# A transformer kernel's first block: the compressed attention branch of all heads computed once, with block matrices, instead of slot by slot

## The reference, cut to what matters

```
# 8 heads of 64 in 2 groups of 4 (H, G); n_cmp = 31
kc = compress(k_cmp, pe_k, w1_k, w2_k)          # [31, H, 64]
vc = compress(v_cmp, pe_v, w1_v, w2_v)
s_cmp = einsum('bshgd,bchd->bhgsc', qg, kc) * 64 ** -0.5
mask_cmp = cmp_start + 31 <= pos                # a block counts once it is complete
p_cmp = masked_softmax(s_cmp, mask_cmp)         # over the 31 blocks
o_cmp = einsum('bhgsc,bchd->bshgd', p_cmp, vc)
...
o_slc, o_win = ...      # both reduce to causal attention over all 512 positions here
o = g[..., 0:1] * o_cmp + g[..., 1:2] * o_slc + g[..., 2:3] * o_win
```

## Time and profile before

| what | us |
|---|---|
| median of three runs | 2639.01 (2637.17 to 2639.22) |
| profiled execution | 2638.98 |
| its span, first to last instruction | 2637.1 |
| TensorE busy | 2595.0 |
| VectorE busy | 1574.9 |
| GpSimd busy | 1525.6 |
| ScalarE busy | 850.3 |

### The profile page before, as it was taken

The page is one execution under the profiler, slowest core; times in us unless marked ns, Lnnn a source line. Parts: engine busy times, 40 slices in busy tenths (PEclk is TensorE's granted clock), DMA queues, the critical chain, the costliest instruction groups (busy, mean ns, idle before and its releaser), DMA issues.

```text
span 2637.1 us, 33257 instructions
## 1 busy us (share of the span) xinstructions
PE 2595.0 (98%) x11819; PEld 2081.2 (79%) x11819; DVE 1574.9 (60%) x2192; ACT 850.3 (32%) x1245; POOL 1525.6 (58%) x1820
## 2 busy tenths in 40 slices
PE   8999999999999999999999999999999999999999
PEld 6777777888888876777888888877677788888887
DVE  6666774388483768755574432657874448443375
ACT  5444444223222332355321111134234532111212
POOL 6634345566665754554566655764454456665576
PEclk9999999999999999999999999999999999999999
DMA  5311112222222221222323222232122232222223
GB/s 194 121 49 57 56 58 103 97 96 96 96 96 98 105 107 64 80 95 81 104 82 111 96 96 95 96 112 86 64 80 96 80 104 96 96 96 96 96 97 126
DMA packets 36832, 247.47 MB, mean 94 GB/s; under 512 B 4464, under 2 KB 4848, under 8 KB 7792
## 3 DMA queue, kind: packets, MB, share of 16 engines
q1 hardware_dynamic: 34704, 238.57, 25.8%
q10 hardware_dynamic: 2016, 7.35, 0.8%
HBM read 243.81 MB, written 2.10 MB: 93 GB/s over the span
## 4 chain that ended last, share of the span: by engine, by line
PE 88%; DVE 9%; ACT 1%; issue 1%; POOL 0%; DMA 0%; DVEq 0%; ACTq 0%
PE bank L745 18%; PE bank L747 17%; PE bank L746 17%; PE both L745 10%; PE both L747 10%; PE both L746 10%; PE bank L780 1%; PE bank L1104 1%; PE both L1080 1%; PE both L932 1%; PE bank L918 1%; DVE small L1411 1%; ACT prob L511 0%; PE bank L956 0%; DVE tb L1847 0%
## 5 line engine op out<-in xcount | busy, mean ns | idle before, releaser
L340 POOL TENSOR_TENSOR w_lo<-raw,w_hi 128x256 fp32r<-128x256 f32 x1784 | 1503.3, 874 | 1021.0 <-ACT w_hi L397 1020.5
L397 ACT ACTIVATE w_hi<-raw 128x1024 fp32r<-128x1024 f32 x446 | 469.3, 1057 | 991.7 <-PE bank L747 496.4
L745 PE MATMUL bank<-a_hi,w_hi 128*128 128x512 f32 x1544 | 633.0, 410 | 4.5 <-POOL w_lo L340 4.5
L747 PE MATMUL bank<-a_hi,w_lo 128*128 128x512 f32 x1544 | 604.2, 391 | 0.0
L746 PE MATMUL bank<-a_lo,w_hi 128*128 128x512 f32 x1544 | 603.7, 391 | 0.0
L745 PEld LDWEIGHTS bank<-a_hi,w_hi 128*128 128x128 f32 x1544 | 291.4, 189 | 75.1 <-issue 12.8
L746 PEld LDWEIGHTS bank<-a_lo,w_hi 128*128 128x128 f32 x1544 | 291.8, 189 | 64.1 <-issue 8.5
L747 PEld LDWEIGHTS bank<-a_hi,w_lo 128*128 128x128 f32 x1544 | 291.0, 188 | 62.8
L745 PE MATMUL bank<-y_hi,w_hi 128*128 128x512 f32 x696 | 272.4, 391 | 0.0
L747 PE MATMUL bank<-y_hi,w_lo 128*128 128x512 f32 x696 | 270.9, 389 | 0.0
L746 PE MATMUL bank<-y_lo,w_hi 128*128 128x512 f32 x696 | 270.8, 389 | 0.0
(11 more groups left out here) (299 smaller groups left out, 3043.5 us busy)
## 6 DMA issues: line engine op xcount, KB each, us to landing
raw<-stream SPq DMA_DIRECT2D x223, 1024.0 KB, 4.8
h<-xT SPq DMA_DIRECT2D x8, 256.0 KB, 6.0
h<-xT ACTq DMA_DIRECT2D x1, 2048.0 KB, 8.1
outT<-h SPq DMA_DIRECT2D x8, 256.0 KB, 2.5
h<-decay ACTq DMA_DIRECT2D x1, 1024.0 KB, 4.8
h<-rope ACTq DMA_DIRECT2D x1, 1024.0 KB, 9.2
prob<-pT ACTq DMA_DIRECT2D x2, 512.0 KB, 4.2
par<-par ACTq DMA_DIRECT2D x2, 408.0 KB, 3.1
```

The costliest lines, as they stand in the source:

```text
L340: pool.tensor_tensor(w_lo[:, s, part], raw[:, s, part], w_hi[:, s, part], ALU.subtract).then_inc(lo_done, 1)
L397: act.activation(w_hi[:, s, cols], raw[:, s, cols], ACT.Copy).then_inc(hi_done, 1)
L745: pe.matmul(dst, w_hi[:, s, cols], rhs_hi(k), start=start and k == 0, stop=False)
L747: ins = pe.matmul(dst, w_lo[:, s, cols], rhs_hi(k), start=False, stop=stop and k == nk - 1)
```

## The change

The compressed branch leaves the slots. In head t = 0 it is computed once for all eight heads:

- `kc` becomes a block matrix 128x64: the keys of group 0 in rows 0 to 63 and columns 0 to 30, those of group 1 in rows 64 to 127 and columns 32 to 62. One product of a full 128-row query tile gives the scores of both groups' heads. 16 such products (4 query blocks x 4 tiles) go at j = 0, k = 1.
- VectorE adds the masks, takes the 32 maxima and subtracts them behind `step_probs(0, 0)` (`compressed_shift`); ScalarE takes one exponential of 128x992 in slot 1; VectorE sums, inverts, masks and gates behind `step_probs(0, 1)` (`compressed_probs`).
- At j = 2, k = 1 TensorE transposes the probabilities (8 transposes), ScalarE copies them in two copies; `vc` holds the values of both groups at four row offsets, and at j = 3 to 6, k = 1 one product of 64 rows and 512 columns gives one t's output for both groups, which ScalarE copies to `cmp_out`.
- `attention_out` adds `cmp_out[:, t]` in one more instruction. The value network's transposes and products move from slot 0 to slot 1.

```diff
@@ TensorE
-                if t == 0:
-                    pe.wait_ge(compressed_keys_ready, 1)
...
-                    pe.matmul(b_cmp[:, 0:NCMP], qt[rows, cols], kc[rows, 0:NCMP], start=True, stop=True)
...
-                    pe.transpose(b_cmp[0:NCMP, 0:P], pc[:, 0:NCMP], ident)\
-                        .then_inc(probs_transposed, ptp.up())
...
-                    pe.matmul(b_o[0:DH, col], vc[:, g * DH:(g + 1) * DH], ptc, start=True, stop=False,
-                              skip_group_check=True)
...
+                def compressed_branch(j):
+                    if j == 0:
+                        pe.wait_ge(compressed_keys_ready, 1)
+                        pe.wait_ge(queries_ready, 1)
+                        pe.wait_ge(hidden_copied, 2)
+                        for i in range(QT):
+                            for q in range(QT):
+                                c0 = i % 2 * 256 + q * 64
+                                ins = pe.matmul((b_r0, b_r1)[i // 2][:, c0:c0 + 64],
+                                                m[:, q + 3, i * P:(i + 1) * P], kc, start=True, stop=True)
+                            if i % 2 == 1:
+                                ins.then_inc(cmp_scores_ready, 1)
+                    if j == 2:
+                        pe.wait_ge(cmp_probs_ready, 1)
+                        for pair, dst in enumerate((b_cmp, b_r0)):
+                            for i in range(QT):
+                                c0 = i * 256 + pair * P
+                                ins = pe.transpose(dst[:, i * P:(i + 1) * P], cmp_rows[:, c0:c0 + P], ident)
+                        ins.then_inc(cmp_transposed, 1)
+                    if 3 <= j < 3 + QT:
+                        q = j - 3
+                        if q == 0:
+                            pe.wait_ge(cmp_probs_copied, 2)
+                            pe.wait_ge(compressed_values_ready, 1)
+                        else:
+                            pe.wait_ge(cmp_out_copied, q)
+                        rows = slice(q % 2 * DH, (q % 2 + 1) * DH)
+                        pe.matmul(b_cmp[:, :], vc[rows, :], cmp_turned[rows, q // 2, :], start=True, stop=True)\
+                            .then_inc(cmp_values_ready, 1)
...
-                    if (t, j) == (0, 0) and k in (2, 5):
-                        (hidden_transposes if k == 2 else compress)(1)
+                    if t == 0 and k == 1:
+                        compressed_branch(j)
+                    if (t, j) == (0, 1) and k == 2:
+                        pe.wait_ge(cmp_scores_read, 2)
+                        hidden_transposes(1)
+                    if (t, j) == (0, 1) and k == 5:
+                        compress(1)
@@ ScalarE
-                    softmax_step([(pc[:, 0:NCMP], b_cmp[:, 0:NCMP], 0),
-                                  (prob[:, 0, 0:n], b_s0[:, 0:n], 1),
-                                  (prob[:, 1, 0:n], b_s1[:, 0:n], 2)], DH ** -0.5)
+                    softmax_step([(prob[:, 0, 0:n], b_s0[:, 0:n], 0),
+                                  (prob[:, 1, 0:n], b_s1[:, 0:n], 1)], DH ** -0.5)
...
+            def compressed_branch(j):        # called behind ahead(u0, j), t == 0
+                if j == 1:
+                    act.wait_ge(cmp_shifted, 1)
+                    act.activation(cmp_seen, cmp_seen, ACT.Exp, scale=DH ** -0.5).then_inc(cmp_exp_ready, 1)
+                if j == 2:
+                    act.wait_ge(cmp_transposed, 1)
+                    act.activation(cmp_turned[:, 0, :], b_cmp[:, :], ACT.Copy).then_inc(cmp_probs_copied, 1)
+                    act.activation(cmp_turned[:, 1, :], b_r0[:, :], ACT.Copy).then_inc(cmp_probs_copied, 1)
+                if 3 <= j < 3 + QT:
+                    act.wait_ge(cmp_values_ready, j - 2)
+                    act.activation(cmp_out[:, j - 3, :], b_cmp[:, :], ACT.Copy).then_inc(cmp_out_copied, 1)
@@ VectorE: step_maxima loses the mask and the maximum of the compressed scores, step_probs its two
@@ instructions on pc
+            def compressed_shift():          # behind step_probs(0, 0)
+                for half, src in enumerate((b_r0, b_r1)):
+                    V.wait_ge(cmp_scores_ready, half + 1)
+                    for o in range(2):
+                        i = 2 * half + o
...
+                        ins = V.tensor_tensor(cmp_seen[:, 8 * i:8 * i + 8, :], x,
+                                              seen.unsqueeze(1).to_broadcast([P, 8, NCMP]), ALU.add)
...
+                V.tensor_reduce(cmp_max, cmp_seen, AX.X, ALU.max).then_inc(vector_step, steps.up())
+                V.wait_ge(vector_step, steps.now())
+                V.tensor_tensor(cmp_seen, cmp_seen, cmp_max.unsqueeze(2).to_broadcast([P, 32, NCMP]),
+                                ALU.subtract).then_inc(cmp_shifted, 1)
+
+            def compressed_probs():          # behind step_probs(0, 1)
+                V.wait_ge(cmp_exp_ready, 1)
+                V.tensor_reduce(cmp_max, cmp_seen, AX.X, ALU.add).then_inc(vector_step, steps.up())
...             # reciprocal of 32, four products with the mask's column, two with the gates
+                V.tensor_tensor(cmp_seen, cmp_seen, cmp_scale.unsqueeze(2).to_broadcast([P, 32, NCMP]),
+                                ALU.mult).then_inc(cmp_probs_ready, 1)
...
@@ attention_out
+                V.wait_ge(cmp_out_copied, t + 1)
+                V.tensor_tensor(out_rows, out_rows, cmp_out[rows, t, :], ALU.add)\
+                    .then_inc(vector_step, steps.up())
+                V.wait_ge(vector_step, steps.now())
@@ slot(t, j)
-                if (t, j) == (0, 0):
+                if (t, j) == (0, 1):
                     hidden_out(1)
                 step_probs(t, j)
                 if (t, j) == (0, 0):
+                    compressed_shift()
+                if (t, j) == (0, 1):
+                    compressed_probs()
                     V.wait_ge(compressed, cp.due())
...             # one copy to vc before; now four, to row offsets 0, 32, 64 and 96
```

More of the change, by code:

```diff
@@ L956, in attention_values @@
                             ins = pe.matmul(b_o[rows, col], v_sw[g][:, a, rows], pt[:, half, a * P:(a + 1) * P],
-                                            start=half == 1 and a == 0, stop=a == i, skip_group_check=True)
+                                            start=a == 0, stop=a == i, skip_group_check=True)
                     ins.then_inc(values_added, pv.up())
@@ L1443, in step_probs @@
                 V.wait_ge(exp_ready, ex.due())
-                V.reciprocal(small[:, 12:15], small[:, 4:7]).then_inc(vector_step, steps.up())
+                V.reciprocal(small[:, 12:14], small[:, 4:6]).then_inc(vector_step, steps.up())
                 V.wait_ge(vector_step, steps.now())
-                gate = [gates[:, i, 3 * g + b:3 * g + b + 1] for b in range(3)]
-                V.scalar_tensor_tensor(out=pc[:, 0:NCMP], in0=pc[:, 0:NCMP], scalar=small[:, 12:13],
-                                       in1=cst[:, K_CMPM + i * NCMP:K_CMPM + (i + 1) * NCMP],
-                                       op0=ALU.mult, op1=ALU.mult).then_inc(vector_step, steps.up())
@@ L1450, in step_probs @@
-                V.tensor_scalar(prob[:, 0, 0:n], prob[:, 0, 0:n], small[:, 13:14], gate[1],
+                gate = [gates[:, i, 3 * g + b:3 * g + b + 1] for b in (1, 2)]
+                V.tensor_scalar(prob[:, 0, 0:n], prob[:, 0, 0:n], small[:, 12:13], gate[0],
                                 ALU.mult, ALU.mult).then_inc(vector_step, steps.up())
-                V.wait_ge(vector_step, steps.now() - 1)
-                V.tensor_scalar(pc[:, 0:NCMP], pc[:, 0:NCMP], gate[0], None, ALU.mult)\
-                    .then_inc(vector_step, steps.up())
@@ new lines, in compressed_probs @@
+            def compressed_probs():
+                V.wait_ge(cmp_exp_ready, 1)
+                V.tensor_reduce(cmp_max, cmp_seen, AX.X, ALU.add).then_inc(vector_step, steps.up())
+                V.wait_ge(vector_step, steps.now())
+                V.reciprocal(cmp_max, cmp_max).then_inc(vector_step, steps.up())
+                V.wait_ge(vector_step, steps.now())
+                for i in range(QT):
+                    c0 = K_CMPM + i * NCMP
+                    V.tensor_scalar(cmp_scale[:, 8 * i:8 * i + 8], cmp_max[:, 8 * i:8 * i + 8],
+                                    cst[:, c0:c0 + 1], None, ALU.mult).then_inc(vector_step, steps.up())
+                V.wait_ge(vector_step, steps.now())
+                for g in range(KVG):
+                    gate = gn[:, :, 12 * g:12 * g + 12].rearrange("p i (q b) -> p i q b", b=3)[:, :, :, 0]
+                    part = cmp_scale.rearrange("p (i q g) -> p i q g", q=QT, g=KVG)[:, :, :, g]
+                    V.tensor_tensor(part, part, gate, ALU.mult).then_inc(vector_step, steps.up())
+                V.wait_ge(vector_step, steps.now())
+                V.tensor_tensor(cmp_seen, cmp_seen, cmp_scale.unsqueeze(2).to_broadcast([P, 32, NCMP]),
+                                ALU.mult).then_inc(cmp_probs_ready, 1)
```

(9 more changed lines are left out.)

68 lines of the change are left out of this document (41 added, 27 removed).

## The result

The changed kernel took 2642.6 us (median of 20 runs, 2637.01 to 2644.78) against 2638.32 us before: a ratio of 1.0014, 95% interval 1.0007 to 1.002. It is 3.7 to 4.3 us slower, inside the 0.2% that I had called no change, and it lies 11 us above the forecast and 5 us above its range. The runs fall into groups by their mean granted clock, the mean over the whole execution of the clock that TensorE was given, as a share of its full speed: three at 2637.0 to 2637.7 have 0.996 to 0.997, the fourteen at 2641.4 to 2642.9 have 0.994, the three above have 0.992 to 0.994.

What follows compares the result with a forecast made beforehand. TensorE, 98% busy, was taken as the bound, with waits for VectorE's queue. From 2639.01 us, -17.1 removed, +9.1 added, +0.5, -1.3, -1.2 and +0.9 for waits and +1.5 for the clock gave -7.6: 2631.4, range 2626 to 2637.5.

Steps and rivals of the forecast that it cites:

- The sign: Whole kernel: forecast faster by 7.6 us; chances 0.65 faster, 0.31 the same, 0.04 slower.
- the score burst: t = 0, j = 0 on TensorE: 16 score products, two instructions each at 0.11, add 3.6 us.
- VectorE's gain in slots 1 and 2: t = 1 to 3: VectorE gains 0.6 us a slot from four removed small instructions at 0.15 each.
- the -1.2 for the wait of L780: Slot 7, all four heads: L780's wait of some 0.3 us for the squares goes, -1.2.
- the clock's 1.5: A clock fall behind the new 1.6 us wait in slot 2 of t = 0 costs +1.5; lower bound 0.
- a rival at 0.1: Burst keeps the clock low, +3.3; falls in later heads' slot 2, 3 x 1.5; +0.2, 2639.2 us; chance 0.1.
- the wait of 3.8: Rival of contended VectorE: slot 2 of t = 0 waits 3.8 us, total -5.4 or less, 2633.6 to 2635; chance 0.13.
- Slot 2 of t = 0 (wait 1.6): VectorE's probabilities at 121.4, TensorE there at 119.8: new wait 1.6 us, older waits of 1.1 gone, +0.5.
- Waits of t = 1 to 3 (-1.3): Of 2.7 us of waits per head 2.2 stay, 0.9 and 1.4 in slots 1 and 2; gain 0.45 x 3.
- A slot's TensorE work: Each of 32 slots loses L929 0.21, L941 0.11 and L951 0.22: 0.54 us a slot, -17.1 in all.
- The values products (L1032): t = 0, j = 3 to 6 on TensorE: one product each at 1.15 us, 4.6 in all.
- The end's wait: End of t = 3: TensorE waits for L1497 behind the new addition, +0.9 us.

Runs made afterwards that it cites:

- e3: Kernel before plus 16 unused products of the score burst's shape ahead of k = 1 of unit (0, 2); 2641.54 us, ratio 1.0012.
- e2: Kernel before plus 16 unused products of the score burst's shape ahead of k = 1 of unit (0, 0); 2645.68 us, ratio 1.0023.
- e1: Changed kernel with the 16 score products spread, four ahead of each of k = 1 to 4 of unit (0, 0); 2638.72 us.
- f1: Changed kernel without the new addition in attention_out, leaving out the compressed branch's share of the output; 2641.84 us.
- f3: Changed kernel with spread score products, an unused exponential per slot, vc copies moved to slot 2 and attention_out's rounding to slot 3; 2627.25 us.
- e4: Changed kernel with one unused 128x31 exponential per slot put back on ScalarE ahead of the other two; 2636.34 us.
- g3: Changed kernel with the removal alone: compressed branch left out altogether, nothing of it computed in t = 0; 2624.96 us.
- f4: f3 with six of the score products ahead of the stage's first wide product, the others at k = 1 to 4; 2625.61 us.
- f2: Changed kernel with both the score products spread over k = 1 to 4 and the unused exponential per slot; 2638.18 us.
- g1: Kernel before with only attention_out's rounding moved from slot 0 to slot 3, the sum in its own tile; 2636.09 us.

## Why the prediction was wrong

The sign was wrong. Three terms failed: the score burst, priced at full clock (3.6; it took 6.7 and kept the clock low for 1.6 more); VectorE's gain in slots 1 and 2, taken as 0.6 each, which was to shorten the waits of t = 1 to 3 and didn't; and the -1.2 for the wait of L780, which stayed. How much later than before the changed kernel stands, at places of the two profiled executions:

| place | after - before | this step | forecast of the step |
|---|---|---|---|
| first wide product, slot (0, 0) | -0.3 | | 0 |
| transposes of slot 2, t = 0 | +10.1 | +10.4 | +4.2 |
| scores of slot 0, t = 1 | +13.2 | +3.2 | +2.5 |
| slot 2, t = 1 / scores of t = 2 | +13.2 / +11.4 | 0 / -1.8 | -1.4 / -3.6 |
| slot 2, t = 2 / scores of t = 3 | +11.4 / +8.1 | 0 / -3.3 | -1.4 / -3.6 |
| slot 2, t = 3 / behind the stage's last wait | +8.1 / +5.7 | 0 / -2.4 | -1.4 / -2.7 |

**The score burst and the clock (term 3.6, and the clock's 1.5).** This step failed worst. I priced the burst at full clock although it stands right behind the wait after which the clock falls, and left the half clock to a rival at 0.1. The burst held TensorE for 6.7, 3.2 more than e3's 3.5; and 15 wide products ran at 0.43 instead of 0.23, three ahead of it and twelve behind, where in the kernel before it was seven (3.2 us at 0.43 each): 8 x 0.2 = 1.6 more. e2 reproduces it (+6.9 in the kernel before), e3 confirms the price for a place where the clock is full, and e1, with the burst spread, has a median 3.9 lower. It is what happens in most executions, not in all: in f1's profile the same burst took 3.5. The rival came near: its sum with the wait of 3.8 is +2.4, with +3.3 for the burst (4.8 measured, 3.2 and 1.6) and three falls in the later heads where one came. That so much of the sum agrees is partly luck. The Trainium skill, "TensorE: Matmul & The Clock Gate", What's actually happening, says that the throttled state is the default and activity releases it. The first half agrees with the fall behind the wait (in f1 and f3 the same wait had none); of the second the rows show less than it promises: TensorE worked 12.80 of 12.80 us behind the fall, and the clock was 0.50 all through.

**Slot 2 of t = 0 (wait 1.6).** The place and the releaser were right, the size was 3.1, and the low stretch behind it came as forecast. Both queues came late, TensorE at 124.1 for 119.8, VectorE at 127.2 for 121.4. Of VectorE's 5.8 beyond the forecast 4.5 was the burst with its low clock, which delayed slot 1's scores to 110.6 for 106.1. The other 1.3 is VectorE's chain from there, 16.6 us for 15.3: the four copies took 0.95 for 0.6, L1499 1.00 for 0.47, and the rest is the smaller gain per slot below. Of the parts of the new work the sums (1.19), the small instructions (0.35, 0.63, 0.27) and the multiplication (1.19) came to 3.7 for 3.8 (in the shift of slot 0 my terms add up to 3.8 and not to the 4.3 that I wrote, and nothing hung on it), and rope_out ran at 0.69 three times as forecast (120.38).

**Waits of t = 1 to 3 (-1.3).** They grew instead: 1.67 and 2.07 in slots 1 and 2 for 0.9 and 1.4. VectorE's gain was read as 0.6 a slot. For slot 1 of t = 2 it was 0.47 (4.79 to 4.32, from the first mask to the first rope product); the small instructions had partly stood in the shadow of larger ones, and four of them gave less than 0.15 each. For slot 2 it was -0.09 (4.77 to 4.86): L1499 took 1.00 for 0.47, the collision of e4. And `attention_out` grew by 1.32, not 0.9: the addition took 1.14, above the top of my row, and the rounding behind it 0.85 for 0.69. Together VectorE gained nothing up to slot 2, and all of TensorE's gain up to there went into waiting: 3 x 1.4. Behind the wait in t = 1 came a fall of 1.5 us, the other half of the clock's rival. I had held a shorter ScalarE for a gain of 0.3 in slot 0; in slot 2 the earlier w_hi cost 0.5.

**The wait of L780 in slot 7 (-1.2).** It was 0.3 in each head, read from start to start, and it is 0.3 still (in t = 1, 261.01 less 260.46 and 0.23): VectorE's sums ahead of it came no earlier against TensorE than before. What did go are the 0.25 ahead of the transposes of slot 7, which is another wait, and the 0.2 of slot 0.

**Right.** A slot's TensorE work: blocks between the units 1.10, 1.53 and 1.96 us for 1.53, 1.96 and 2.39, and 0.11 for the transpose, 0.54 a slot together. The values products (L1032) add 1.15 each, at 134.43 and in the next three slots; the transposes 0.8 for 0.9. The end's wait 0.95 longer for 0.9. For the removal alone I expected 19 us ahead of g3 (17.1, 1.1 of waits in t = 0 and 1 of the others); it gave 13.4. Two falls of the clock in its profile are about 3.0 of the 5.6 between, the wait of L780 1.2 and the wait left in slot 2 of t = 0 0.9.

Between the forecast's -7.6 and the span's +5.9 lie 13.5 us: 6.2 up to slot 2 of t = 0; 0.7 in the rest of that head, 0.3 of it L780's; in t = 1 to 3 4.2 for the waits, 1.5 for the fall in t = 1 and 0.9 for L780. That makes 13.5, with 0.3 to either side for what the places leave out. Open is when the clock falls. The length of the wait doesn't decide it alone: one of 2.0 to 2.1 us is followed by the low clock and the next, as long, isn't. With it stays open why the runs of one such kernel lie up to 8 us apart (2637.01 to 2644.78) where those of f4 lie within 1.4; f1's profile shows one way, the burst at full clock in one execution and at half in others.

## What to carry to other kernels

Price an added TensorE burst at the clock that its place has, and look there first for the wait that the clock falls behind: the same 16 unread products made the kernel 2.8 us slower in one slot and 6.9 in another. Where TensorE waits for another engine's queue, count a saving on TensorE only up to the wait, and count what is saved or added on that queue from a whole slot's start-to-start time, not from the removed instructions' durations. Removing a short instruction on a third engine moves everything behind it; look for the two engines that then start at the same moment.

## What the runs showed of the hardware

- A float32 product of 128x128 weights and 64 columns (two instructions) takes 0.22 us at the full granted clock (e3: 3.5 for 16) and 0.42 at the low one (e2 and the change: 6.7); one instruction of a wide product takes 0.23 and 0.43.
- A burst of 16 such products behind a fall went with a low clock for 12.8 us in the change and in e2 and for 10.2 in e4, against 3.2 with mostly wide products there; in f1 the burst ran at full clock. In groups of four among wide ones the wide ones were back at full clock 4.8 us behind the wait in e1 (94.95 to 99.72) and 6.9 in f2 (94.32 to 101.22).
- In slots 1 to 7 no profile has a low stretch behind a wait of 1.7 us or less; behind 2.0 to 2.1 it came in some heads (209.8 in the change, 277.7 and 353.5 in f1) and not in others; behind the 2.4 to 3.1 of t = 0 it came in all six profiles that have such a wait. The stage's ends differ: behind 1.44 at its start it came (the kernel before, e2, e3, g1), behind 2.02 it did not in f1 and f3, and behind 2.73 at its end it did not in e1, f2 and f3.
- A VectorE product of 128x384 with one tile as input took 0.48 us when it started 0.12 us or more ahead of w_hi's end, which releases GpSimd, 0.94 to 1.01 when it started 0.01 to 0.08 behind it, and where the two are equal within 0.01 either: 0.47 in the kernel before (273.38) and g1, 1.01 in f1 (119.86).
